# Sixteen quads of weight blocks by Strassen's seven products in a two-layer encoder trunk

## What is computed

```
for layer in range(2):
    h = rms_norm(x, norm_w[layer])
    z = h @ w_in              # 4096 x 13312 in layer 0, 4096 x 10240 in layer 1
    q, k, v, gate = split(z)  # layer 0: heads A (global) and B (neighbourhood)
    y = attention(q, k, v) * silu(gate)
    x = x + y @ w_out         # 4096 x 4096
return rms_norm(x, final_norm_w)
```

## Time and profile before

| what | us |
|---|---|
| three runs, median (lowest to highest) | 2814.05 (2813.85 to 2814.28) |
| the profiled execution, its time | 2814.37 |
| the profiled execution, its span | 2812.6 |
| PE busy | 2797.6 (99%) |
| DVE busy | 1687.7 (60%) |
| ACT busy | 1347.7 (48%) |

### The profile page before, as it was taken

The page is one execution under the profiler, slowest core; times in us unless marked ns, Lnnn a source line. Parts: engine busy times, 40 slices in busy tenths (PEclk is TensorE's granted clock), DMA queues, the critical chain, the costliest instruction groups (busy, mean ns, idle before and its releaser), DMA issues.

```text
span 2812.6 us, 37759 instructions
## 1 busy us (share of the span) xinstructions
PE 2797.6 (99%) x12681; PEld 2329.4 (83%) x12681; DVE 1687.7 (60%) x2103; ACT 1347.7 (48%) x1654; POOL 16.4 (1%) x14
## 2 busy tenths in 40 slices
PE   9999999999999999999999999999999999999998
PEld 7888888888888888888888888888888888888886
DVE  7766666556556555566665556666655666665554
ACT  6455455445444444444443445555544455543333
POOL 0000000000000000000000000000000000000000
PEclk9999999999999999999999999999999999999999
DMA  9777777777767777677777767777676777676665
GB/s 334 222 210 232 225 226 221 224 217 228 234 209 215 228 220 239 189 254 254 253 240 222 223 211 218 231 233 220 221 226 204 231 227 225 216 251 218 215 209 187
DMA packets 357923, 637.17 MB, mean 227 GB/s; under 512 B 25376, under 2 KB 79136, under 8 KB 357792
## 3 DMA queue, kind: packets, MB, share of 16 engines
q1 hardware_dynamic: 343824, 593.52, 67.7%
q10 hardware_dynamic: 13968, 41.95, 4.1%
HBM read 585.56 MB, written 49.81 MB: 226 GB/s over the span
## 4 chain that ended last, share of the span: by engine, by line
PE 99%; DMA 0%; issue 0%; DVE 0%; ACT 0%; POOLq 0%; POOL 0%; SPq 0%; DVEq 0%; ACTq 0%
PE proj L1098 32%; PE proj L1099 32%; PE proj L1100 32%; PE o_ps L1099 1%; PE o_ps L1098 1%; PE sc_ps L1100 1%; PE o_ps L1100 1%; PE sc_ps L1099 1%; PE sc_ps L1098 1%; DMA raw<-in_w_in_ab 0%; DVE w_lo L757 0%; DVE x_fin L1091 0%; ACT w_hi L637 0%; POOLq L268 0%; POOL rms L598 0%
## 5 line engine op out<-in xcount | busy, mean ns | idle before, releaser
L757 DVE TENSOR_TENSOR w_lo<-raw,w_hi 128x1024 fp32r<-128x1024 f32 x990 | 1208.5, 1221 | 856.7 <-ACT w_hi L637 850.5
L637 ACT ACTIVATE w_hi<-raw 128x1024 fp32r<-128x1024 f32 x990 | 1049.6, 1060 | 1148.6 <-PE proj L1100 1087.3
L1098 PE MATMUL proj<-w_hi,h_hi 128*128 128x512 f32 x2936 | 1143.4, 389 | 2.0 <-issue 1.5
L1099 PE MATMUL proj<-w_lo,h_hi 128*128 128x512 f32 x2936 | 1142.8, 389 | 0.0
L1100 PE MATMUL proj<-w_hi,h_lo 128*128 128x512 f32 x2936 | 1142.1, 389 | 0.0
L1100 PEld LDWEIGHTS proj<-w_hi,h_lo 128*128 128x128 f32 x2936 | 551.2, 188 | 114.9
L1098 PEld LDWEIGHTS proj<-w_hi,h_hi 128*128 128x128 f32 x2936 | 551.4, 188 | 114.5 <-issue 2.4
L1099 PEld LDWEIGHTS proj<-w_lo,h_hi 128*128 128x128 f32 x2936 | 551.4, 188 | 109.9
L1098 PE MATMUL proj<-w_hi,y_hi 128*128 128x512 f32 x1024 | 398.4, 389 | 0.0
L1099 PE MATMUL proj<-w_lo,y_hi 128*128 128x512 f32 x1024 | 398.4, 389 | 0.0
L1100 PE MATMUL proj<-w_hi,y_lo 128*128 128x512 f32 x1024 | 398.3, 389 | 0.0
(11 more groups left out here) (115 smaller groups left out, 975.5 us busy)
## 6 DMA issues: line engine op xcount, KB each, us to landing
raw<-in_w_in_ab SPq DMA_DIRECT2D x414, 512.0 KB, 4.4
raw<-in_w_in_c SPq DMA_DIRECT2D x320, 512.0 KB, 4.4
raw<-in_w_out_ab SPq DMA_DIRECT2D x128, 512.0 KB, 4.5
raw<-in_w_out_c SPq DMA_DIRECT2D x128, 512.0 KB, 4.5
head_turn<-head_stage SPq DMA_DIRECT2D x256, 96.0 KB, 1.9
head_land<-head_turn ACTq DMA_DIRECT2D x64, 384.0 KB, 5.5
landing<-group_turn ACTq DMA_DIRECT2D x31, 512.0 KB, 5.5
group_turn<-q_stage SPq DMA_DIRECT2D x64, 128.0 KB, 3.2
```

What stands on the lines that cost most here:

```text
L637: nc.scalar.activation(w_hi[:, slot], raw[:, slot], ACT.Copy).then_inc(hi_ready, 1)
L757: nc.vector.tensor_tensor(w_lo[:, slot], raw[:, slot], w_hi[:, slot].bitcast(F32), ALU.subtract) \
L1098: nc.tensor.matmul(dst, hi, r_hi, start=start, stop=False)
L1099: nc.tensor.matmul(dst, hi, r_lo, start=False, stop=False)
```

## The change

Eleven pairs get one or two **quads**: four blocks that make up a 2 x 2 matrix of weight blocks (two row blocks c1 and c2 by both groups), against the 2 x 2 matrix of activations (two token tiles by the same rows). Instead of 8 products of a tile, 48 matmuls, PE does 7 of them, 42 matmuls (`quad`), by Strassen's scheme in Winograd's form. For this
- DVE makes four mixes of raw weights in each quad (`quad_lo`), and ACT and DVE split seven operands instead of four (`quad_hi`); four of these use the ring's slots and three the spare slots in rows of tiles that are not in use;
- DVE makes four sums of activation tiles once for each row pair and stage (`make_sums`, at the steps in `combine`, 7 times);
- three products go to banks of their own (m1, m6, and m7 in the bank of `o_ps`), and seven additions (`fold`) bring them into the four banks. ACT copies m1 to SBUF first (`copy_m1`), at the step behind the last quad; two folds and then three stand in this step and the next, and two where group 1 begins (`second_at`). PE waits for the first five there.

Where quads stand in the 32 blocks: in three `vg` pairs, two `x1` pairs and one `x2` pair one quad at blocks 12 to 15, with 2 blocks of group 0 behind it; in the x1 pair between those, two `qg` pairs and one `x2` pair two quads, at 5 and 13, with 3 blocks behind the second; in the last pair two, at 3 and 11, also with 3. Pairs with quads finish group 0 ahead of group 1. Loops that held such pairs are unrolled or shortened, and the split of the key turn moves from step 5 to step 9.

```diff
+def with_quads(first, second, end=()):
+    blocks, quads = [], {}
+    for e in first:
+        if isinstance(e, tuple):
+            c1, c2 = e
+            quads[len(blocks)] = e
+            blocks += [(0, c1), (1, c1), (1, c2), (0, c2)]
+        else:
+            blocks.append((0, e))
+    return blocks + [(1, c) for c in second] + list(end), quads
+REST1, REST2 = [0, 1, *range(4, KC // 2)], [0, 1, *range(6, KC // 2)]
+VG_QUADS = with_quads([*REST1[:12], (2, 3), *REST1[12:]], REST1)
+X1_QUADS = with_quads([*REST1[:12], (2, 3), *REST1[12:]], REST1)
+TWO_QUADS = with_quads([*REST2[:5], (2, 3), *REST2[5:9], (4, 5), *REST2[9:]], REST2)
+LAST_QUADS = with_quads([*REST2[:3], (2, 3), *REST2[3:7], (4, 5), *REST2[7:-2]], REST2[:-2],
+                        [(g, EARLY + c) for g in range(2) for c in range(LATE)])
...
-K_NORM_TURN, K_TURN = (0, 5, 7, 10), (0, 0, 2, 5)
+K_NORM_TURN, K_TURN = (0, 5, 7, 10), (0, 0, 2, 9)
...
-        (1, [Pair("in_ab", vg(0), "vg", "qk", "qk", v=1)]),
-        (3, [Pair("in_ab", qk(1), "qk", "B", "vg", batch=4), Pair("in_ab", vg(1), "vg", "qk", "qk", v=2)]),
+        (1, [Pair("in_ab", vg(0), "vg", "qk", "qk", v=1, quads=VG_QUADS, heads=16, combine=((5, "vg", 0, 2),))]),
+        (2, [Pair("in_ab", qk(1), "qk", "B", "vg", batch=4),
+             Pair("in_ab", vg(1), "vg", "qk", "qk", v=2, quads=VG_QUADS, heads=20, heads_step=4)]),
+        (1, [Pair("in_ab", qk(3), "qk", "B", "vg", batch=6)]),
+        (1, [Pair("in_ab", vg(3), "vg", "qk", "qk", v=4)]),
...
-        (3, [Pair("out_ab", out_cols(1), "x1", "h", "x1", x_batch=0)]),
-        (1, [Pair("in_c", kvc(0), "kv", "h", "x1", x_batch=3)]),
-        (1, [Pair("in_c", c(0), "qg", "k", "kv", v=5)]),
+        (1, [Pair("out_ab", out_cols(1), "x1", "h", "x1", x_batch=0, quads=X1_QUADS, heads=32,
+                  combine=((6, "x1", 0, 2), (26, "x1", 1, 4)))]),
+        (1, [Pair("out_ab", out_cols(2), "x1", "h", "x1", x_batch=1, quads=TWO_QUADS, heads=32)]),
+        (1, [Pair("out_ab", out_cols(3), "x1", "h", "x1", x_batch=2, quads=X1_QUADS, heads=32, spare="x1_end")]),
+        (1, [Pair("in_c", kvc(0), "kv", "h", "x1", x_batch=3, combine=((15, "qg", 0, 2), (19, "qg", 1, 4)))]),
+        (1, [Pair("in_c", c(0), "qg", "k", "kv", v=5, quads=TWO_QUADS, heads=32)]),
...
+        (1, [Pair("out_c", out_cols(1), "x2", "none", "x2", quads=X1_QUADS, heads=64,
+                  combine=((6, "x2", 0, 2), (26, "x2", 1, 4)))]),
+        (1, [Pair("out_c", out_cols(2), "x2", "none", "x2", quads=TWO_QUADS, heads=64)]),
+        (1, [Pair("out_c", out_cols(3), "x2", "none", "x2", quads=LAST_QUADS, heads=64)]),
...
+                    if b >= RING and p.quad_at(b - RING) is not None and p.quad_at(b - RING)[2] < 3:
+                        k, _, part = p.quad_at(b - RING)
+                        sp.wait_ge(mixed, QUAD * (p.quad_n + k) + part + 1)
+                    elif b >= RING:
+                        sp.wait_ge(lo_ready, p.o + p.freed[b - RING])
+                    elif p.n0 > 0:
+                        sp.wait_ge(lo_ready, p.o + b - RING + 1)
...
+            def quad_hi(p, k, start, part):
+                n = p.o + p.op[start]
...
+                def hi(r, source, count=1):
+                    if r % 2 == 0:
+                        act.wait_ge(block_done, slot_free_after(p, start + r // 2))
+                    elif r == 5:
+                        act.wait_ge(block_done, n + 2)
+                    elif earlier is not None:
+                        act.wait_ge(block_done, earlier + (6 if r == 1 else 4))
+                    elif r == 1:
+                        act.wait_ge(block_done, p.o)
+                        act.wait_ge(folded, p.folds)
+                        act.wait_ge(sums_split, p.combined + (1 if p.combine else 0))
+                    dst, _ = weights_of(p, start, r)
+                    nc.scalar.activation(dst, source, ACT.Copy).then_inc(hi_ready, count)
+                if part == 0:
+                    raw_landed(p, start)
+                    hi(0, b11)
+                if part == 1:
+                    raw_landed(p, start + 2)
+                    hi(1, b22)
+                if part == 2:
+                    act.wait_ge(mixed, mixes_done + 1)
+                    hi(2, mix[:])
+                    act.wait_ge(mixed, mixes_done + 2)
+                    hi(3, mix3[:])
+                if part == 3:
+                    raw_landed(p, start + 3)
+                    hi(4, b21)
+                    act.wait_ge(mixed, mixes_done + 3)
+                    hi(5, mix[:])
+                    act.wait_ge(mixed, mixes_done + 4)
+                    hi(6, b21, 2)
+            def copy_m1(p, b):
+                if p.quads and b == p.last_quad + QUAD:
+                    act.wait_ge(folded, p.folds)
+                    act.wait_ge(block_done, p.o + p.op[p.last_quad] + OPS)
+                    nc.scalar.activation(folds_of(p)[0], m1[:], ACT.Copy).then_inc(m1_copied, 1)
...
+                    sums_hi_at(p, b)
+                    copy_m1(p, b)
                     if p.n0 == 0 and b + AHEAD < NB and p.blocks[b + AHEAD][0] == 0:
                         first_x(p.blocks[b + AHEAD][1])
                     split_hi_at(p, b)
...
+            def quad_lo(p, k, start, part):
+                n = p.o + p.op[start]
+                mix, mix3 = (tile[:] for tile in mix_of[p.out])
+                mixes_done = QUAD * (p.quad_n + k)
+                b11, b12, b22, b21 = (raw[:, (start + r) % RING] for r in range(QUAD))
+                minus = lambda dst, a, b: nc.vector.tensor_tensor(dst, a, b, ALU.subtract)
+                def lo(r, source, count=1):
+                    hi, dst = weights_of(p, start, r)
+                    dve.wait_ge(hi_ready, n + r + 1)
+                    minus(dst, source, hi.bitcast(F32)).then_inc(lo_ready, count)
+                if part == 0:
+                    lo(0, b11)
+                if part == 1:
+                    second = (start + 1) % RING
+                    dve.wait_ge(raw_loaded[second], 16 * (p.n * (NB // RING) + (start + 1) // RING + (second > 1)))
+                    dve.wait_ge(lo_ready, n + 1)
+                    minus(mix, b12, b11).then_inc(mixed, 1)
+                    lo(1, b22)
+                if part == 2:
+                    dve.wait_ge(mixed, mixes_done + 1)
+                    minus(mix3, b22, b12).then_inc(mixed, 1)
+                    lo(2, mix)
+                    dve.wait_ge(mixed, mixes_done + 2)
+                    dve.wait_ge(lo_ready, n + 3)
+                    minus(mix, b22, mix).then_inc(mixed, 1)
+                    lo(3, mix3)
+                if part == 3:
+                    lo(4, b21)
+                    dve.wait_ge(mixed, mixes_done + 3)
+                    dve.wait_ge(lo_ready, n + 5)
+                    minus(b21, b21, mix).then_inc(mixed, 1)
+                    lo(5, mix)
+                    dve.wait_ge(mixed, mixes_done + 4)
+                    lo(6, b21, 2)
+                    dve.wait_ge(lo_ready, n + OPS)
+            def make_sums(p, b):
+                for k, (at, stage, quad, c1) in enumerate(p.combine):
+                    if b not in (at, at + 1):
+                        continue
...
+            def fold(p, b):
+                add = lambda dst, a, b: nc.vector.tensor_tensor(dst, a, b, ALU.add).then_inc(folded, 1)
+                (x11, x21), (x12, x22) = [[bank[:] for bank in group] for group in proj]
+                f1, f2, f3 = folds_of(p)
+                if b == p.last_quad + QUAD:
+                    dve.wait_ge(m1_copied, p.pair_w + 1)
+                    dve.wait_ge(block_done, p.o + p.op[p.last_quad] + OPS)
+                    add(f2, m6[:], f1)
+                    dve.wait_ge(folded, p.folds + 1)
+                    add(f3, m7[:], f2)
+                if b == p.last_quad + QUAD + 1:
+                    dve.wait_ge(folded, p.folds + 2)
+                    add(f2, x22, f2)
+                    dve.wait_ge(folded, p.folds + 3)
+                    add(x22, x22, f3)
+                    add(x12, x12, f2)
+                if b == p.second_at:
+                    dve.wait_ge(block_done, p.o + p.op[p.second_at])
+                    add(x11, x11, f1)
+                    add(x21, x21, f3)
+                    dve.wait_ge(folded, p.folds + FOLDS)
 
...
+                if p.quads and b == p.second_at:
+                    pe.wait_ge(folded, p.folds + 5)
+                elif c == 0 and p.n0 > 0:
...
+            def quad(p, k, start, part):
+                n = p.o + p.op[start]
...
+                def times(r, left, dst, first, final, count=1):
+                    right_hi, right_lo = weights_of(p, start, r)
+                    pe.wait_ge(lo_ready, n + r + 1)
+                    for j, (a_hi, a_lo) in enumerate(left):
+                        last = three_passes(dst[:], a_hi, a_lo, right_hi[:, j], right_lo[:, j],
+                                            first and j == 0, final and j == 1)
```

(16 more changed lines are left out.)

258 lines of the change are left out of this document (207 added, 51 removed).

## The result

The changed kernel takes 2826.78 us, the median of five runs (2824.22 to 2832.74); the ratio to the kernel before is 1.0047, with a 95% interval of 1.0035 to 1.006. So it is slower, by 12.7 us in the medians, where the prediction had 2821, 7 us slower (and a range of 2807 to 2831). The execution that was profiled is the longest of the five: 2832.74 us with a span of 2830.9.

A forecast was written before the change was run, and what follows sets the result against it. PE bounds the kernel: time is matmul count times spacing. New waits of 16.2 (folds), 8.9 (x1 pair with two quads) and 4.5 (smaller ones), 29.6 us, less 22.5 saved, give +7.1 on 2814.05: 2821 us, range 2807 to 2831.

The forecast's parts named there:

- The sign: Whole kernel: predicted slower, by 7.1 us; chances slower 0.65, same 0.19, faster 0.16.
- six fold waits: First block of group 1, six single-quad pairs: PE waits 2.7 us each for the fifth fold, 16.2 us in all.
- clock behind them: Behind the six fold waits: nothing in the sum; as a rival, one block at half clock each, 2837 us, chance 0.04.
- x1 pair with two quads: Turn work and late raw tiles delay low halves: 2.9 us first quad, 3.0 block 11, 3.0 second quad; 8.9 in all.
- last pair, its quads: Last pair: first quad right behind `add_x2` loses 1.7 us; second quad's raw loads share the queue with a residual load, 0.5.
- x2 pair before it: Second-last pair: quad at block 5 hidden; folds, `add_x2` and a `w_lo` end 1.1 us late; residual load beside second quad, 0.5.
- c pairs: Sums and later turn lie in DVE's idle time, no cost; up to 1 us each if raw tiles land later than 4.4.
- sums ahead of the vg and x1 quads: DVE's activation sums shortly before the first vg and first x1 quad leave them 0.3 and 0.4 us late.
- 96 matmuls and the back edges: Sixteen quads save 96 matmuls, 21.8 us; one loop back edge goes, 0.8 with the other; together 22.5 us saved.
- Q+8.15: Q is PE's end of the quad; the fifth fold was to end 8.15 us later, with PE coming at 5.44 in six pairs.
- P+12.6: P is PE's start of the x1 pair with two quads; `split_turn` was to start 12.6 us later and take 2.1.
- the third rival: Raw loads fall behind: a quad's loads bunch up and land late, about 1.4 us at eight places; 2832 us, chance 0.15.

The follow-up runs named there:

- the folds first: Changed kernel with, on DVE, the folds in the two steps behind a pair's last quad put ahead of that step's low half: 2806.86 us.
- the folds by bank: One-quad-per-pair kernel, all folds ahead of low halves; PE starts group 1 after the fourth fold, waiting for the fifth only before its second matmul group: 2799.69 us.

## Why the prediction was right, and where it was not

The sign, and the folds as its cause, were right. The terms, as costs by the starts, in the two profiled executions of the changed kernel:

| term | forecast | 2832.7 us | 2824.5 us |
|---|---|---|---|
| six fold waits | 16.2 | 15.0 | 15.0 |
| clock behind them | 0 | 8.4 | 3.4 |
| x1 pair with two quads | 8.9 | 5.2 | 6.2 |
| last pair, its quads | 2.2 | 2.5 | 2.2 |
| x2 pair before it | 1.6 | 4.5 | 3.5 |
| c pairs | 0 | 3.4 | 2.4 |
| sums ahead of the vg and x1 quads | 0.7 | 0.8 | 0.2 |
| 96 matmuls and the back edges | -22.5 | -23.8 | -23.8 |

The sums are +16.0 and +9.1; with what the first 35 us took more (1.4 and 0.1) and 1 us of wider spacing elsewhere they come to the 18.4 and 10.2 us that the spans grew.

**Removed.** Right. 96 matmuls are gone, 21.8 us. The two stalls on "issue" cost 1.0 us each by the starts and not 0.76, and neither shows in the trace of after. That is partly luck: one of 1.3 us came back in the experiment that kept PE busy. DVE was busy for 1893.3 us and ACT for 1406.5, where 1905 and 1414 were given.

**Folds.** Right to 0.4 us. The steps had the fifth fold end at Q+8.15; it ends at 604.81, Q+7.8, and PE starts at 604.96, Q+7.94. Six waits of 2.5 us where 2.7 was forecast, none in the pairs with three blocks behind. That the two low halves in front are the cause is shown: one moved takes 1.1 us off, both moved 2.2.

**The clock.** This is the step that failed. The forecast listed it as a rival with a chance of 0.04, "one block at half clock behind each of six folds". The mechanism was right, and both its chance and its price were off: it happens behind two to five of the six waits, and costs 1.7 us each time, not 2.7. I had no row with a wait of this length and took that for a reason to leave the term out of the sum; it was a reason to put a part of it in. With half of the six at 1.7 the forecast would have been 2826. The Trainium skill (TensorE: Matmul & The Clock Gate, section HAM oscillation — how this bites in real kernels) has a PE kept waiting fall back to half clock; here the trace agrees in five of six waits and in two of six, with the granted clock at 0.51 in the stretch at 604.9. The waits in the Trainium skill's example there are longer, some 3 to 5 us; here 2.5 were enough in 7 of 12, and the measurement decides.

**The x1 pair with two quads.** The first quad was to lose 2.9 us and lost 1.9: `split_turn` began at P+11.9 and not P+12.6 (P is 1371.33, `add_x1`'s start less 0.5, as in the earlier trace rows). The 3.0 us at block 11 did not come. The second fetch left at P+21.4, 1.8 earlier than forecast, and its `h_hi` began only 4.0 us later, where the earlier trace rows had 6.6 and 5.8; `split_turn` was over at 1400.6, P+29.3, in time for block 11. The second quad lost 3.3, as forecast 3.0, and for the reason given: a raw tile asked for at 1401.9 landed 5.0 us later. The term was 8.9, and 5 to 6 came.

**The c pairs and the x2 pair before the last.** The forecast had, for the x2 pair, "the quad is at block 5 and stays hidden" and 0.5 for each residual load, and nothing for the c pairs unless a raw tile took more than 4.4 us. They did: 7.9 us behind a residual load, and 7.4 and 5.2 in the second c pair. Here I took the median of the landings where the rows had 3.5 to 7.1, though the tile for the first spare slot is asked for only when the block four ahead of it is split. The c pairs, given as 0, cost 3.4 and 2.4 us in the two executions; the second quad of the x2 pair, given as 0.5, cost 3.2 and 2.1; and the quad at block 5 ahead of it was not hidden (0.7 and 0.9). These terms were in the third rival, raw loads that fall behind (2832), which is thus part of what happened. That late raw tiles are the cause is shown in the last two x2 pairs, by the late residual loads; for the c pairs it is read from the chain, and no run moved a load there.

The surplus of 5.7 us over the forecast in the medians is then the clock (3.4 to 8.4) and the raw tiles (4 to 6 more than given), less what the x1 pair did not lose (3 to 4) and what the six waits and the saving were better than given (1.2 and 1.3). That the sum came out within 6 us is luck in part: its errors had both signs.

What is not settled: whether the clock falls behind a given wait of 2.5 us. It did at the first vg pair and the last x1 pair in both profiles and at the third vg pair in neither, and two profiles don't tell a rule.

## What to carry to other kernels

When work moves from the bounding engine to a helper, write down for each hand-back in what order the helper does it beside its regular work; here two instructions of 1.2 us, not urgent and merely in front, turned a gain of 0.25% into a loss of 0.5%. Give a saving a place where the helper and its loads have rebuilt their lead: eleven quads, one late in each pair, took 2803.0 us where sixteen took 2806.9, both with the folds first, and thirteen, with the folds by bank too, 2796.1. And price a wait of PE of some 2 us or more with a part of a clock fall behind it.
